# Router scores in two halves of tokens, p's product over three places of the program, and the shared down products around four PSUM banks

## What is computed

```
h = layer_norm(x)                                   # first stage
proj = h @ w_in                                     # then a gated branch A and an attention branch B
merged = sigmoid(g_a) * (y_a @ w_branch_a) + sigmoid(g_b) * (y_b @ w_branch_b)
h = layer_norm(ALPHA * h + merged @ w_out)          # "out stage"
scores = sigmoid(h @ router_w)                      # 64 experts, top 8 picked per token
shared = (silu(h @ sh_gate) * (h @ sh_up)) @ sh_down
routed = sum over the 8 picked experts of w * ((silu(h @ w_gate[e]) * (h @ w_up[e])) @ w_down[e])
r = ALPHA * h + routed + shared
r = r + sigmoid(r @ ple_w_gate) * (p @ ple_w_proj)  # p: 512 x 256, ple_w_proj: 256 x 1024
out = layer_norm(r)
```

## Time and profile before

| | |
|---|---|
| median of 3 runs | 1084.4 us (1083.57 to 1086.21) |
| the profiled execution, its own time | 1084.34 us |
| its span in the trace | 1082.4 us |
| PE busy | 1060.6 us (98%) |
| DVE, ACT, POOL busy | 853.9 us, 729.5 us, 247.2 us |
| mean granted TensorE clock | 0.996 |

### The profile page before, as it was taken

The page is one execution under the profiler, slowest core; times in us unless marked ns, Lnnn a source line. Parts: engine busy times, 40 slices in busy tenths (PEclk is TensorE's granted clock), DMA queues, the critical chain, the costliest instruction groups (busy, mean ns, idle before and its releaser), DMA issues.

```text
span 1082.4 us, 15808 instructions
## 1 busy us (share of the span) xinstructions
PE 1060.6 (98%) x5362; PEld 862.4 (80%) x5362; DVE 853.9 (79%) x900; ACT 729.5 (67%) x836; POOL 247.2 (23%) x177
## 2 busy tenths in 40 slices
PE   8999999999999989999999999999999999999996
PEld 5888877778878767888888888888888888888585
DVE  6834345662455788999999999999999999998576
ACT  4621235452233547889988888988888998888644
POOL 1000000000003221333333333333333333332321
PEclk9999999999999999999999999999999999999999
DMA  9542222114351978999999999999999999999931
GB/s 329 206 156 78 78 78 65 53 41 154 117 205 58 366 283 321 365 388 386 383 384 386 393 377 387 390 388 388 387 383 377 390 382 388 383 395 323 299 148 61
DMA packets 73581, 300.83 MB, mean 278 GB/s; under 512 B 14913, under 2 KB 17985, under 8 KB 48578
## 3 DMA queue, kind: packets, MB, share of 16 engines
q1 hardware_dynamic: 54256, 263.51, 61.6%
q0 software_dynamic: 19008, 35.71, 12.8%
q10 hardware_dynamic: 274, 1.05, 0.2%
HBM read 287.08 MB, written 46.66 MB: 308 GB/s over the span
## 4 chain that ended last, share of the span: by engine, by line
PE 93%; DMA 3%; DVE 2%; issue 1%; ACT 1%; SPq 0%; DVEq 0%; POOLq 0%; ACTq 0%
PE ps L470 27%; PE ps L472 26%; PE ps L471 26%; PE ps L1632 5%; PE ps L1656 1%; DMA odd_rows<-y,put_idx 1%; PE ps L865 1%; PE ps L889 1%; PE ps L876 1%; PE ps L568 1%; DMA p_w<-in_ple_w_proj 1%; DVE w_lo L454 1%; ACT w_hi L432 1%; PE ps L728 1%; PE ps L361 1%
## 5 line engine op out<-in xcount | busy, mean ns | idle before, releaser
L1897 DVE TENSOR_TENSOR w_lo<-gu_raw,w_hi 128x2048 fp32r<-128x2048 f32 x128 | 292.6, 2286 | 5.0 <-ACT w_hi L1741 5.0
L1741 ACT ACTIVATE w_hi<-gu_raw 128x2048 fp32r<-128x2048 f32 x128 | 245.1, 1915 | 3.2 <-DMA gu_raw<-in_moe_w_up 3.2
L470 PE MATMUL ps<-w_hi,xgT_hi 128*128 128x512 f32 x512 | 200.5, 392 | 4.9 <-issue 4.9
L472 PE MATMUL ps<-w_hi,xgT_lo 128*128 128x512 f32 x512 | 200.3, 391 | 0.0
L471 PE MATMUL ps<-w_lo,xgT_hi 128*128 128x512 f32 x512 | 199.9, 390 | 0.0
L1902 DVE TENSOR_TENSOR dn_lo<-dn_raw,dn_hi 128x2048 fp32r<-128x2048 f32 x62 | 142.1, 2292 | 19.7 <-ACT dn_hi L1750 19.2
L1750 ACT ACTIVATE dn_hi<-dn_raw 128x2048 fp32r<-128x2048 f32 x62 | 118.8, 1916 | 0.0
L470 PEld LDWEIGHTS ps<-w_hi,xgT_hi 128*128 128x128 f32 x512 | 96.5, 188 | 26.0 <-issue 6.0
L472 PEld LDWEIGHTS ps<-w_hi,xgT_lo 128*128 128x128 f32 x512 | 96.5, 189 | 20.1
L471 PEld LDWEIGHTS ps<-w_lo,xgT_hi 128*128 128x128 f32 x512 | 96.4, 188 | 19.9
L2002 POOL DMA_INDIRECT xg<-h_rows,get_idx x64 | 67.8, 1060 | 173.5 <-ACT get_idx L1768 135.6
(11 more groups left out here) (234 smaller groups left out, 1950.7 us busy)
## 6 DMA issues: line engine op xcount, KB each, us to landing
gu_raw<-in_moe_w_gate SPq DMA_DIRECT2D x64, 1024.0 KB, 11.6
gu_raw<-in_moe_w_up SPq DMA_DIRECT2D x64, 1024.0 KB
dn_raw<-in_moe_w_down SPq DMA_DIRECT2D x62, 1024.0 KB
raw<-in_w_in SPq DMA_DIRECT2D x17, 1024.0 KB, 5.1
h_rows<-x_rows SPq DMA_DIRECT2D x8, 512.0 KB, 3.2
raw<-in_w_out SPq DMA_DIRECT2D x4, 1024.0 KB, 5.0
ple_raw<-in_ple_w_gate SPq DMA_DIRECT2D x4, 1024.0 KB, 13.0
x_rows<-in_x SPq DMA_DIRECT2D x4, 512.0 KB, 12.2
```

Source lines behind the costliest of these rows:

```text
L470: nc.tensor.matmul(out, x_hi, w_hi, start=first, stop=False)
L472: return nc.tensor.matmul(out, x_lo, w_hi, start=False, stop=last)
L1741: nc.scalar.activation(m.w_hi[:, 2 * x.b + half], m.gu_raw[:, 2 * x.b + half], ACT.Copy).then_inc(gu_hi, 1)
L1897: nc.vector.tensor_tensor(m.w_lo[:, 2 * x.b + half], m.gu_raw[:, 2 * x.b + half], m.w_hi[:, 2 * x.b + half].bitcast(F32), ALU.subtract).th ...
```

## The change

- `Projection`: units 0 to 2 are in the first stage (p's rows and `ple_w_proj` are now loaded behind token tile 1), units 3 and 4 around the first `turn_x`, units 5, 6 and 7 in expert steps 0 and 1. The parts are stored by three more issues. ACT takes their copies in steps 0 and 1, and has two waits for earlier stores of this product and, in step 3, one for the last.
- `Routing.score` takes 256 tokens at a time: the first half ahead of `gate_up` of tile 0, the second in its place behind it. The shared gate and up products, the sigmoid, `scale_rows`, `times_up` and the weight splits of the first two experts are in a new order. The out stage turns its tiles through two pairs of banks.
- Piece 13 is split behind attention pair 1 and no more ahead of the attention; ACT takes an early Sigmoid of one element, which loads its table; piece 24 is split right behind gate 15.
- The first stage has 14 more short matmuls without use (`stay_busy`) and another order on ACT.
- The shared down products of the end go around banks 1, 2, 0, 7 where they went around 0 and 1.

The diff, cut to its core:

```diff
 class Projection:
-    TURN, MAIN = (2, 4), ((1, 2), (5, 6))
+    EARLY, MID = 3, 4
+    FIRST_TILE, BANK = (0, 1), (2, 7, 2, 6, 5, 6, 5, 6)
...
     def term(self, pe, u, j):
...
-            if u % 4 >= 2:
+            if u not in (0, 1, 3, 4):
                 pe.wait_ge(self.copied, u - 1)
...
+    def store_early(self, sp):
+        sp.wait_ge(self.copied, self.EARLY)
+        sp.dma_start(self.pp_rows[0:P, :].rearrange("p (c n) -> p c n", c=2), self.m.pp_early[:, 0:2]).then_inc(self.stored, 16)
+        sp.dma_start(self.pp_rows[P:2 * P, 0:512], self.m.pp_early[:, 2]).then_inc(self.stored, 16)
+    def store_mid(self, act):
+        act.wait_ge(self.copied, self.MID)
+        act.dma_start(self.pp_rows[P:2 * P, 512:D], self.m.pp_mid[:]).then_inc(self.stored, 16)
+    def store_late(self, act):
+        act.wait_ge(self.copied, 2 * NT)
+        act.dma_start(self.pp_rows[2 * P:, :].rearrange("(t p) n -> p t n", p=P), self.m.pp_late[:]).then_inc(self.stored, 16)
...
-    SPLIT_AFTER_PAIR = {6: (14,), 7: (15,), 8: (16,), 14: (17,), 15: (18, 19)}
-    SPLIT_AFTER_GATE = {10: (20,), 11: (21,), 12: (22,), 14: (23,)}
+    SPLIT_AFTER_PAIR = {1: (13,), 6: (14,), 7: (15,), 8: (16,), 14: (17,), 15: (18, 19)}
+    SPLIT_AFTER_GATE = {10: (20,), 11: (21,), 12: (22,), 14: (23,), 15: (24,)}
...
         load_rows(0)
         norm.load_gain(sp, a["ln_in_g"])
-        projection.load_rows(sp, 0)
         ring.load_half(sp, 0)
-        projection.load_weights(sp, 0)
         ring.load_half(sp, 1)
         load_rows(1)
+        projection.load_rows(sp, 0)
+        projection.load_weights(sp, 0)
...
             first_terms(0, True, hi0)
+            projection.unit(pe, 0)
...
             first_terms(0, False, hi0)
-            projection.unit(pe, 2)
+            projection.unit(pe, 1)
             norm.turn(pe, between)
...
-            projection.unit(pe, 3)
...
         pe.wait_ge(constants_set, 1)
+        stay_busy(14)
+        norm.turn(pe, 0)
         projection.turn(pe, 0)
         stay_busy(8)
-        norm.turn(pe, 0)
-        projection.unit(pe, 0)
-        projection.unit(pe, 1)
         first_unit(1)
+        projection.unit(pe, 2)
...
+        nc.scalar.activation(m.peak[:], m.eps[:], ACT.Sigmoid)
         ring.split_hi(act, 12)
-        ring.split_hi(act, 13)
...
-    norm = RowNorm(nc, m, ps, norm_semaphores, banks=(0,))
+    norm = RowNorm(nc, m, ps, norm_semaphores, banks=(0, 3))
...
         pe.wait_ge(norm_semaphores.lo_done, norm.before + 2)
-        routing.gate_up(pe, 0)
+        pe.wait_ge(added, 2 * NT - 1)
+        routing.score(pe, 0)
+        routing.gate_up(pe, 0, 0, 4)
         norm.turn(pe, NT - 1)
-        routing.gate_up(pe, 1, 0, 4)
+        routing.gate_up(pe, 0, 4, 7)
         pe.wait_ge(norm_semaphores.lo_done, norm.before + NT)
...
-    def score(self, pe):
+    def score(self, pe, half):
+        cols = slice(half * 2 * P, (half + 1) * 2 * P)
...
     def step(x, at=99):                                # TensorE
...
+                if first and at == 0:
+                    projection.unit(pe, 5)
+                    projection.term(pe, 6, 0)
+                if first and at == 1:
+                    projection.term(pe, 6, 1)
+                    projection.unit(pe, 7)
...
     def step(x, at=99):                                # ScalarE
...
+                if first and at == 3:
+                    act.wait_ge(projection.stored, 64)
...
+                if first and at == 0:
+                    act.wait_ge(projection.stored, 48)
                 silu(x)
                 split_x(x.next(1))
+                if first and at == 0:
+                    projection.copy(act, 5)
...
                     split_hT(x.next(-1))
                     if first and at == 1:
+                        projection.copy(act, 6)
+                        projection.copy(act, 7)
+                        projection.store_late(act)
                         act.wait_ge(routing.h_stored, 16)
-                        act.wait_ge(projection.stored, 32)
                     split_down(x.next(-1))
...
-    MAIN, TURN, PT = (0, 1), (3, 5), (7, 0)
+    MAIN, TURN, PT, SHARED = (0, 1), (3, 5), (7, 0), (1, 2, 0, 7)
...
-            if u >= 2:
-                pe.wait_ge(self.h_out, u - 1)
+            if u >= 4:
+                pe.wait_ge(self.h_out, u - 3)
```

More of the change, by code:

```diff
@@ L538, in load_rows @@
     def load_rows(self, sp, part):
-        rows = self.a["p"][0, 0][part * 2 * P:(part + 1) * 2 * P, :]
+        first = self.FIRST_TILE[part]
+        rows = self.a["p"][0, 0][first * P:(first + 2 + part) * P, :]
         sp.dma_start(self.m.p_part[part][:], rows.rearrange("(t p) d -> p t d", p=P)).then_inc(self.rows_in, 16)
@@ L679, in sync @@
         sp.dma_start(m.sg_b[:], a["sg_b_s"][0].rearrange("g i -> (g i)").partition_broadcast(P)).then_inc(small_in, 16)
[L680 removed]
+        projection.store_early(sp)
         norm.store(sp, 2, h0)
@@ L1723, in tensor @@
             locate_part(Expert(0, 0, q), ROW_COLS + 8 * q, 0, rows_located)
+        routing.gate_up(pe, 3, 1, KD)
         pe.wait_ge(routing.h_ready, 2)
+        projection.term(pe, 3, 0)
+        turn_x(Expert(0, 0, 0))
+        projection.term(pe, 3, 1)
         projection.unit(pe, 4)
-        projection.unit(pe, 5)
-        projection.term(pe, 6, 0)
-        turn_x(Expert(0, 0, 0))
         pe.wait_ge(routing.weighed, 1)
@@ L1731, in tensor @@
             locate_part(Expert(0, 0, q), WEIGHT_COLS + 8 * q, 3, located)
-        projection.term(pe, 6, 1)
-        projection.unit(pe, 7)
         rounds(pe, body, embedding.tensor, late=True)
@@ L1835, in scalar @@
         split(Expert(0, 0, 0), 0)
+        split(Expert(0, 0, 0), 1)
         routing.row_norm.high_part(act, NT - 1)
-        split(Expert(0, 0, 0), 1)
+        routing.scale_rows(act, 0)
+        routing.sigmoid(act)
         routing.silu(act, 0)
-        for t in range(3):
-            routing.scale_rows(act, t)
-        routing.sigmoid(act)
+        routing.scale_rows(act, 1)
         routing.silu(act, 1)
+        projection.copy_rows(act, 1)
+        routing.scale_rows(act, 2)
         routing.scale_rows(act, 3)
         routing.silu(act, 2)
-        projection.copy_rows(act, 1)
         routing.silu(act, 3)
         split(Expert(0, 0, 1), 0)
+        split_x(Expert(0, 0, 0))
+        projection.copy(act, 3)
+        projection.store_mid(act)
+        split(Expert(0, 0, 1), 1)
         projection.copy(act, 4)
-        split(Expert(0, 0, 1), 1)
-        projection.copy(act, 5)
-        split_x(Expert(0, 0, 0))
-        projection.copy(act, 6)
-        projection.copy(act, 7)
-        projection.store(act, 1)
         rounds(act, body, embedding.scalar)
@@ L1976, in vector @@
         one_hot(Expert(0, 0, 1))
+        routing.times_up(dve, 2)
         find_rows()
-        routing.times_up(dve, 3)
+        split(Expert(0, 0, 0), 1)
         routing.weigh(dve)
@@ L2040, in gpsimd @@
         pool.wait_ge(*routing.rows_stored)
+        pool.wait_ge(projection.turned, 2)
         early.clear(pool, 2)
```

103 lines of the change are left out of this document (53 added, 50 removed).

## The result

The changed kernel takes 1092.27 us (median of 5 runs, 1091.19 to 1093.41), beside 1086.21 (5 runs, 1083.57 to 1088.22) for the kernel before on the same chip: ratio 1.0058, 95% interval 1.0039 to 1.0078. It is slower by 0.6%.

The account below looks back on a forecast made before the run. TensorE, busy for 98% of the span, was taken as the bound, so only its holes could be won. 1084.34 - 0.4 - 0.8 - 1.0 - 2.0 + 1.1 = 1081.2 us, range 1078.7 to 1084.5.

Parts of the forecast that it names:

- Routing: 2.0 us: From scores to expert 0: earlier scores and picks, the gather wait filled, expert 0 starting 2.0 us early.
- the clock rival: Low clock behind new waits of TensorE, 1.6 us per fall: one fall chance 0.22, two 0.11, all three 0.07.
- its terms ahead: Gains forecast ahead of routing: first stage 0.4 us, ahead of the attention 0.8, behind the last gate 1.0.
- the row store landed when forecast: Routing: the row store, with 256 KB less ahead of it in the queue, lands another 0.6 us sooner.
- The wait at `count`: Routing: TensorE reaches `count` before the picks, a new wait of 1.9 us.
- First stage: 0.4 us won: First stage: one unit of p's product leaves, at most 1.67 us, mostly held back by a weight piece; 0.4 won.
- Attention and gates: 1.8 won: Waits for the first sigmoid and, behind the last gate, for a weight piece's low part go: 0.8 and 1.0 us.
- Expert steps 0 to 3: 1.1 lost: Both holes filled and low clock gone, but ACT's late `dn_hi` delays DVE and expert 3: 1.1 us lost.
- End: nothing: Last stage: shared products lose two PSUM waits, but tile 0's turn waits some 1.9 us for x_rows; nothing won.

Follow-up runs that it names:

- 1: Changed kernel with only DVE's low-part split of expert 0's second weight half moved back early, ahead of the logits' copy: 1083.24 us, ratio to kernel before 0.9986.
- experiment 2: Changed kernel, split left late, SyncE held until both gathers land before loading expert 2's second half and storing residual rows: 1085.34 us, ratio to kernel before 1.0002.
- experiment 3: Kernel of 1 with SyncE's load of expert 2's second half and residual stores held until the gather lists are written: 1090.68 us, ratio to kernel before 1.0057.
- 4: Kernel before with only DVE's split of expert 0's second weight half moved behind find_rows: 1093.78 us, ratio to kernel before 1.0074.
- experiment 10: Kernel before with the edits of attention and gates alone (pieces 12, 13, 24, early sigmoid table load): 1084.40 us, ratio to kernel before 0.9990.
- 8: Kernel of 1 with ScalarE making the down weights' high part ahead of p's copies 6 and 7 in step 1: 1082.75 us, ratio to kernel before 0.9982.
- experiment 11: Kernel of 1 with ScalarE's copies of p's units 6 and 7 and their store moved into expert step 2: 1086.63 us, ratio to kernel before 1.0010.
- 7: Kernel of 1 with the shared down products back on two banks: 1083.27 us, ratio to kernel before 0.9979.
- experiment 6: Kernel of 1 with only the 1 MB load of expert 2's second half held until the gather lists are written: 1085.51 us, ratio to kernel before 1.0001.
- 5: Kernel of 1 with only the 2 MB of residual stores held until the gather lists are written: 1084.74 us, ratio to kernel before 1.0005.

## Why the prediction was wrong

Forecast 1081.2, range 1078.7 to 1084.5; measured 1092.3, outside it and of the other sign.

- **The step that failed** is in "Routing: 2.0 us": "its wait of 0.75 us for the gather is filled", and so "Expert 0 begins at 391.3, 2.0 us early". I took the gather's duration over from before, 3.8 us, with only its start moved. DVE's `split(E0,1)` was moved past the logits, the picks and `find_rows`, and I asked what TensorE and ACT would wait for, not which transfers the split releases. It releases 1 MB, and 2 MB queued behind it. Shown by experiments 1 to 4. From the kernel with the line early to the changed one expert 0 moves by 7.2 us. The gather is 6.0 us longer (9.78 less 3.80): 1.0 of it is GpSimd's longer issue (experiment 2), 5.0 the traffic (4.8 by experiment 3). It is issued 0.2 later, and the stretch from the first turn to expert 0, at the low clock, takes 1.5 more (5.33, in 1 3.79). Less 0.5 that TensorE had to spare with the early split (385.57, where a gather of 3.8 us ends at 385.06), that is 7.2. No rival of mine had this place; the clock rival had the mechanism of its last part.
- **The rest of the routing was right.** With the split early expert 0 starts at 389.36. The forecast, with its terms ahead (391.3 less 2.2), was 389.1. The two halves of the scores take 5.6 us (5.8). The picks arrive at 376.54; forecast 378.3 less 2.2, 376.1. That the row store landed when forecast (364.65; 367.48 less 0.6 and 2.2 is 364.7) is in part luck: it was issued only 1.1 us sooner than before, not 2.2, and took 7.3 us where 9.1 stood before and 8.5 was counted. The wait at `count` is 1.3 us (1.9).
- **First stage: 0.4 us won by the forecast, 0.4 lost as measured.** The unit starts at 25.74 (25.80 before), but with a slow first matmul, and tile 1's turn follows at 28.92, 28.54 before. p's rows arrive behind the weight piece, TensorE has 0.57 us of wait for them, and the terms that moved forward run at half pace: 1.85 us from the first of four to what follows (13.43 to 15.28), 0.46 each where 0.23 is usual. The trace shows the granted clock at 1.00 there, so the cause stays open.
- **Attention and gates: 1.8 won by the forecast**, 1.71 measured in experiment 10. In the changed kernel 1.07 is left at the scores, since 0.4 went in the first stage and 0.3 is a rest of the wait for `w_lo` (0.28 at 314.23), about as foreseen (0.2).
- **Expert steps 0 to 3: 1.1 lost by the forecast, 2.0 as measured** (31.75; before 29.77, 423.03 less 393.26). Both holes are filled, no low clock follows, `dn_hi` is late and DVE idles 3.2 us for it, all as written. I had expert 3 at 30.8. Of the 0.95 that it is later, 0.8 is there at `dn_hi`: that starts 21.1 us behind expert 0 (417.71), where I had 20.3, and `split_x(3)` 30.4 (427.02), where I had 29.6. Half of it comes from TensorE (expert 2 at 19.4, not 19.0, with the wait of 0.56 for `onehot` in step 0 that I had left out), half from ScalarE (1.7 us from there for the last copy and the issue, where I had 1.3). So the links behind `dn_hi` held, but they are not the only ones: experiments 8 and 11 show that all of ScalarE's work ahead of expert 3's high parts counts, not only that ahead of `dn_hi`. The wait itself stands in two places, 1.3 us at `found` and 0.66 ahead of expert 3, where I had one of 2.3.
- **End: nothing by the forecast, 2.9 lost as measured** (8.2 at the main product, 5.3 at expert 3). TensorE was to stand there for 1.9 us and stood for 3.0, with the low clock behind it: 3.97 us from the turn to the main product, 2.32 before, 1.65 more, where a rival had 1.6. That the x_odd load took 1.1 us more than before is not explained; in kernels with the same end it took 4.57 to 6.64, so part of these 2.9 us may be this one execution's. The medians are 6.1 apart, not 8.3.

Sum against the kernel before (minus is won): -1.1 until the scores, -3.3 to the picks, +7.7 to expert 0, +2.0 to expert 3, -0.2 to the shared products, +3.0 behind them: 8.1, beside 8.2 measured at the main product.

The version with the split early (1), also with two banks (7) or the down split first (8), is the fastest of the study, 1082.75 to 1083.27 us: 0.14 to 0.21% under the kernel before (the intervals of 7 and 8 end below 1, that of 1 at 1.0000). That is less than the forecast's 3.2 us and within 0.3%.

## What to carry to other kernels

When an instruction is moved later, follow its semaphore into every queue, the transfer queues first: list what it releases, and what is queued behind that. Then look for the latency-bound transfer (a gather, a small load on the critical path) that stands at the new time. A transfer's duration from the old trace holds only as long as the DMA share around it does; here the same gather took 3.8 us with only 512 KB beside it and 9.8 (1.0 of it GpSimd's longer issue) beside 3 MB of SyncE's, though the DMA engines had been idle right ahead of it.

## What the runs showed of the hardware

- The gather of one expert's rows took 3.80 us from issue to landing with a store of 512 KB issued 0.5 us ahead of it (kernel before), 4.81 with a 1 MB load issued 0.8 us ahead of it (experiment 6), 5.92 with 2 MB of stores (5), 8.62 with both (3). This doesn't grow evenly; no run here shows why. The Trainium skill, "DMA: Bandwidth & Descriptors", section "Issuing engines are not separate DMA queues", says that transfers of all issuing engines run on the same 16 DMA engines and interleave. The traces agree that they meet. The same page of the Trainium skill, section "SWDGE vs HWDGE vs iDMA", has each DMA engine go round-robin between its queues. No run here shows the order inside an engine.
- GpSimd's issue of the first gather took 2.31 us in the three kernels where DVE's 2.28 us subtraction was already running when it began (the changed one, 2 and 4) and 1.09 in all others, and the gather of experiment 2 took 1.0 more with it at no traffic. The later gathers follow the same pattern in all fourteen traces: each issue that begins while such a subtraction runs ends 0.9 to 1.0 us behind the subtraction's end (in the kernel before 2.51 us, 397.84 to 400.35, beside one that ends at 399.48), and one that begins just ahead of such a subtraction is not longer (1.05 us at 917.72, the subtraction from 917.73). No experiment changed this alone.
- A matmul of 256 columns took 0.115 us, half of the 0.230 at 512, with 64 columns of weights.
- A 1 MB store issued into the experts' weight loads took 12.3 us to land (experiment 11); at its place in the changed kernel it took 6.4.
